# The first norm's root applied behind the input projection, with x and the first unit's weights loaded in column blocks

## What is computed

```python
xn = rmsnorm(x, norm_mix)     # x * rsqrt(mean(x*x, -1) + 1e-6) * gain: one root per token
p = xn @ w_in                 # 2048 x 6400, 52 MB of weights
pA, pB, pC, pD = split(p)     # 1792, 1536, 1536, 1536 columns
pA = pA + (shift_right(pA) - pA) * mu          # token shift, then split in r, k, v, w_lo, a_lo, g_lo
decay = f(tanh(w_lo) @ w2 + w0); a = sigmoid(a_lo @ a2 + a0); g = sigmoid(g_lo) @ g2
kk = k * k_k; kk = kk / max(sqrt(sum(kk*kk) per head), 1e-12)
yA = rwkv7 scan(r, decay, k, v, kk, a) * g     # computed in chunks of 64 tokens
yB = band attention(pB); yC = differential attention(pC); yD = b * conv3(c * h)   # pD = b, c, h
x = x + concat(yA, yB, yC, yD) @ w_out
x = x + mixture of 32 experts(rmsnorm(x))      # 201 MB of expert weights
return rmsnorm(x, norm_final)
```

## Time and profile before

| | |
|---|---|
| median of three runs | 940.85 us (940.47 to 941.32) |
| the profiled execution, its own time | 940.73 us |
| its span, from the first to the last instruction | 938.8 us |
| mean granted clock of TensorE, as a share of full speed | 0.926 |
| busy: PE | 787.3 us (84%) |
| busy: DVE | 432.1 us (46%) |
| busy: ACT | 280.6 us (30%) |
| busy: POOL | 73.5 us (8%) |
| read from HBM | 280 MB, 303 GB/s over the span |

### The profile page before, as it was taken

How to read it: one execution, slowest core, us unless ns; L and a number is a source line. 1 busy time by engine, 2 the same in 40 slices (tenths; PEclk the granted TensorE clock), 3 DMA queues, 4 the chain that set the end, 5 groups by cost and what they waited for, 6 DMA issues and landing times.

```text
span 938.8 us, 18498 instructions
## 1 busy us (share of the span) xinstructions
PE 787.3 (84%) x8182; PEld 634.4 (68%) x8182; DVE 432.1 (46%) x709; ACT 280.6 (30%) x458; POOL 73.5 (8%) x79
## 2 busy tenths in 40 slices
PE   7999999999999999999999774686646856559654
PEld 7999999999999999888877452353523534236322
DVE  6758947654676576854552513113231122311403
ACT  6455543433355666455510101000010000100014
POOL 3110003241000100600000000000000000000002
PEclk9999999999999999999999978797887978979878
DMA  9695544334344545999899999999999999999995
GB/s 302 208 284 159 177 134 137 120 110 135 108 147 153 148 147 180 349 347 365 287 341 404 427 427 429 427 426 428 427 427 427 427 429 426 426 428 427 427 403 203
DMA packets 84655, 285.83 MB, mean 304 GB/s; under 512 B 3818, under 2 KB 55284, under 8 KB 72156
## 3 DMA queue, kind: packets, MB, share of 16 engines
q1 hardware_dynamic: 82304, 278.93, 77.0%
q0 software_dynamic: 1568, 4.02, 1.7%
q10 hardware_dynamic: 700, 1.65, 0.5%
HBM read 280.37 MB, written 4.22 MB: 303 GB/s over the span
## 4 chain that ended last, share of the span: by engine, by line
PE 59%; DMA 33%; DVE 3%; ACT 2%; issue 1%; SPq 1%; POOL 1%; ACTq 0%; POOLq 0%; DVEq 0%
PE bank L1046 26%; DMA arena<-in_expert_w_up 12%; DMA arena<-in_expert_w_down 10%; DMA arena<-in_expert_w_gate 9%; PE bank L1510 8%; PE bank L1590 3%; PE bank L1063 3%; PE bank L1065 3%; PE bank L1064 3%; PE bank L965 2%; PE bank L1475 2%; DMA arena<-in_norm_final 1%; PE bank L1209 1%; DVE ring_r L1715 1%; PE bank L1016 1%
## 5 line engine op out<-in xcount | busy, mean ns | idle before, releaser
L1046 PE MATMUL bank<-xTr,hi 128*128 128x256 f32 x1280 | 235.7, 286 | 0.3 <-DVE ring_r L1715 0.2
L1510 PE MATMUL bank<-arena 128*32 128x256 f32 x2048 | 144.0, 449 | 104.5 <-DMA arena<-in_expert_w_up 60.8
L1046 PEld LDWEIGHTS bank<-xTr,hi 128*128 128x128 f32 x1280 | 199.2, 192 | 5.4 <-issue 3.3
L1715 DVE TENSOR_TENSOR ring_r<-arena,hi 128x1024 fp32r<-128x1024 f32 x132 | 161.9, 1236 | 88.0 <-ACT hi L654 85.5
L1510 PEld LDWEIGHTS bank<-arena 128*32 128x32 f32 x2048 | 80.3, 129 | 165.8 <-issue 138.4
L1046 PE MATMUL bank<-xTr,ring_r 128*128 128x256 f32 x640 | 181.0, 283 | 0.0
L654 ACT ACTIVATE hi<-arena 128x1024 fp32r<-128x1024 f32 x132 | 138.9, 1062 | 111.5 <-PE bank L1046 84.1
L1046 PEld LDWEIGHTS bank<-xTr,ring_r 128*128 128x128 f32 x640 | 122.7, 192 | 0.0
L2149 DVE TENSOR_TENSOR arena<-arena,bank 128x512 f32<-128x512 f32 x56 | 57.8, 1092 | 75.2 <-PE bank L1486 75.2
L895 ACT ACTIVATE g<-bank,coef 128x256 f32<-128x256 f32 x8 | 3.8, 473 | 256.0 <-PE bank L1510 256.0
L1590 PE MATMUL bank<-arena,const 128*32 128x512 f32 x448 | 54.6, 643 | 14.4 <-DMA arena<-in_expert_w_down 14.4
(11 more groups left out here) (338 smaller groups left out, 884.6 us busy)
## 6 DMA issues: line engine op xcount, KB each, us to landing
arena<-in_expert_w_gate SPq DMA_DIRECT2D x30, 2048.0 KB, 30.1
arena<-in_expert_w_up SPq DMA_DIRECT2D x29, 2048.0 KB, 31.8
arena<-in_w_in SPq DMA_DIRECT2D x50, 1024.0 KB, 5.3
arena<-in_expert_w_down SPq DMA_DIRECT2D x24, 2048.0 KB, 30.1
arena<-in_w_out SPq DMA_DIRECT2D x16, 1024.0 KB, 6.0
arena<-in_expert_w_down SPq DMA_DIRECT2D x16, 512.0 KB, 9.1
arena<-in_expert_w_down SPq DMA_DIRECT2D x8, 1024.0 KB, 15.6
arena<-in_expert_w_up SPq DMA_DIRECT2D x6, 1024.0 KB, 7.1
```

Source lines behind the costliest of these rows:

```text
L1046: ins = MM(PJ[n % 2][:, h * U:(h + 1) * U], a, b, start=h + q + tt + k == 0, stop=h == 1 and q == 3 and tt == 3 and k == 2)
L1510: ins = MM(gu[slots_of(a), u * EH:(u + 1) * EH], xg[:, t, slots_of(a)], slot(NUQ * h + NCG * u + a)[:, t * EH:(t + 1) * EH], start=t == 0, ...
L1715: TT(ring_r[:, n % 2, q, :], ring[:, n % 2, q, :], hi[:, g % NHI, :].bitcast(f32), ALU.subtract).then_inc(s["lo_done"], 1)
```

## The change

**At the start.** SP loads the identity first (ScalarE did before), then x in four blocks of 512 columns over all 256 tokens, and behind each block the quarter of unit 0's weights that goes with it (before: three loads of x, then two halves of unit 0). x is no longer scaled. TensorE has 52 fillers, no longer 78, and transposes each block of x when it lands: two blocks ahead of granule 0, one behind granule 0 and one behind granule 1. The gain is loaded and transposed by itself; the other parameters are transposed behind unit 0.

**The root.** The four passes that square x now stand behind unit 0's splits: on both engines between splits 4, 5 and 6. GpSimd issues its eleven loads first, when the transposes are done, and takes the roots after that. VectorE multiplies the identity by the roots (`diag`), and TensorE multiplies a matrix of ones by the result behind granule 5, which gives each token's root in every partition; VectorE copies that to R.

**Applying it.** Bank n is copied to SBUF (`raw` for units 0 to 6), and GpSimd multiplies it by R in place (`scale(n)`), for units 0 to 6, for the q and k parts of both attentions, and for part of D. For the four units that lie with tokens on the partitions the copy itself takes the root as its scale, in two halves. For three units of D VectorE's copy multiplies by R. `keep` and `mix` of units 0 to 6 now read `raw` in SBUF, behind GpSimd, and each stands one or more splits later; `mix` has its own split ahead of it. Nothing changes in the projection's matmuls, in w_out, or in the experts.

The core of the diff:

```diff
@@ SP
-            sp.dma_start(xs[:, 0, :], x_v[0]).then_inc(x_ld[0], 16)
-            for n, part in ((1, slice(0, DM // 2)), (2, slice(DM // 2, DM))):
-                sp.dma_start(xs[:, 1, part], x_v[1][:, part]).then_inc(x_ld[n], 16)
+            sp.dma_start(const[:, 0:P], A["const"][:, 0:P]).then_inc(const_ld, 16)
+            for q in range(4):
+                cols_ = slice(q * 512, (q + 1) * 512)
+                sp.dma_start(xs[:, :, cols_], x_cols[:, :, cols_]).then_inc(x_ld[q], 16)
+                sp.dma_start(ring[:, 0, q, :].rearrange("p (t c) -> p t c", t=4),
+                             w_in_v[:, 4 * q:4 * q + 4, order[0] * U:(order[0] + 1) * U]).then_inc(part_ld[q], 16)
@@ GpSimd
+            pool.wait_ge(s["xt_ready"], 8)
+            for dst, src in loads:
+                pool.dma_start(dst, src).then_inc(par_ld, 16)
             rsqrt(st[:, 0:1])
             rsqrt(st[:, 1:2])
-            for dst, src in loads:
-                pool.dma_start(dst, src).then_inc(par_ld, 16)
+            def scale(n):
+                pool.wait_ge(s["pj_evac"], n + 1)
...
+                    by = R[:, :].unsqueeze(1).to_broadcast([P, 2, SEQ])
+                step(G.tensor_tensor(t, t, by, ALU.mult), s["pj_scaled"])
@@ ScalarE
             def keep(n):
-                act.wait_ge(s["gran_used"], 4 * n + 4)
+                act.wait_ge(s["pj_scaled"], n + 1)
...
-                    A_(mA[:, i, :], PJ[n % 2][:, h * SEQ:(h + 1) * SEQ], ACT.Copy,
+                    A_(mA[:, i, :], raw[n % 2][:, h, :], ACT.Copy,
...
+            for q in range(4):
+                x_high(2 * q)
+                x_high(2 * q + 1)
+                split_hi()
+            split_hi()
+            square(0)
+            split_hi()
+            square(1)
+            split_hi()
@@ TensorE
-            warm(26)
...
+            x_block(0)
+            x_block(1)
             for q in range(4):
                 first_high(q)
                 first_low(q)
-                if q == 0:
-                    x_transpose(7, 0)
-                    x_transpose(7, 1).then_inc(s["xt_ready"], 1)
+                if q < 2:
+                    x_block(q + 2)
...
-            granules(4)
+            granules(2)
+            pe.wait_ge(s["diag_done"], NM)
+            pe.wait_ge(s["pool_ones"], 3)
+            for m in range(NM):
+                ins = MM(K[2][:, m * P:(m + 1) * P], ones_f, diag[:, m, :], start=True, stop=True)
+            ins.then_inc(s["ones_ps"], 1)
+            granules(2)
@@ VectorE
             def mix(n):
+                split_lo(1)
                 for h in range(2):
...
-                    step(STT(mA[:, i, 1:], PJ[n % 2][:, h * SEQ:(h + 1) * SEQ - 1], mu[:, i:i + 1], mA[:, i, 1:],
+                    step(STT(mA[:, i, 1:], raw[n % 2][:, h, 0:SEQ - 1], mu[:, i:i + 1], mA[:, i, 1:],
                              ALU.mult, ALU.add), s["mixA"])
```

More of the change, by code:

```diff
@@ L383, in store_x2 @@
                 sp.dma_start(x2_cols[:, :, nb * 512:(nb + 1) * 512], x2b[nb % 3]).then_inc(x2_st[nb], 16)
-            for n in range(NU_IN + NU_OUT):
+            for n in range(1, NU_IN + NU_OUT):
                 for half in range(2):
@@ L525, in _ @@
             pool.dma_start(gnb[:, :], bc(A["rwkv_gn_b"][0])).then_inc(par3_ld, 16)
+            for n in range(3, NA + 2):
+                scale(n)
             pool.wait_ge(s["gram_ev"], 8)
@@ L545, in _ @@
                      s["gnw_done"])
-            for m in range(NM):
-                rsqrt(st[:, 24:32])
+            for n in (9, 10, 13, 14):
+                scale(n)
+            rsqrt(st[:, 24:32])
+            scale(15)
+            rsqrt(st[:, 24:32])
+            scale(16)
             pool.wait_ge(s["sm_done"], sm_count(NBH - 1))
@@ L552, in _ @@
             pool.dma_start(rw[:, :, NGR:36], A["router_expert_w"].rearrange("l (t p) g -> p (l t) g", t=KT)).then_inc(par2_ld, 16)
-            for i in range(NCH):
+            scale(19)
+            scale(20)
+            rsqrt(cst[:, :, 1:2])
+            scale(21)
+            for i in range(1, NCH):
                 rsqrt(cst[:, :, 1:2])
-            pool.wait_ge(s["pj_evac"], 3 + 19 - NA)
             b_, c_, h_ = (Dq[:, 0, i] for i in range(3))
@@ L696, in _ @@
                         bias=w0h[:, c:c + 1], scale=0.5), s["lora_ev"])
+            keep(2)
             for c in range(AT):
@@ L702, in _ @@
             advance(4)
-            keep(3)
+            evac(3)
             step(A_(lam[:, 2:4], lam[:, 0:2], ACT.Exp), s["lam_exp"])
@@ L722, in _ @@
             advance(1)
+            evac(5)
+            advance(1)
             keep(5)
+            advance(3)
+            evac(6)
+            advance(1)
+            keep(6)
             advance(4)
-            keep(6)
-            advance(5)
             for i in range(6):
@@ L1716, in split_lo, with square @@
                        ALU.subtract).then_inc(s["lo_done"], 1)
+                    if q == 3 and NA + 15 <= n - 1 < NU_IN - 1:
+                        evac(n - 1)
+            def square(h):
+                half = slice(h * DM // 2, (h + 1) * DM // 2)
+                step(V.tensor_tensor_reduce(xsq[:, 1, half], xs[:, 1, half], xs[:, 1, half], 1.0, 0.0, ALU.mult, ALU.add,
+                                            st[:, 1 + 2 * h:2 + 2 * h]))
             def mix(n):
+                split_lo(1)
                 for h in range(2):
@@ L1722, in mix @@
                     v.wait_ge(s["mix1"], 2 * n + 2)
-                    step(STT(mA[:, i, 1:], PJ[n % 2][:, h * SEQ:(h + 1) * SEQ - 1], mu[:, i:i + 1], mA[:, i, 1:],
+                    step(STT(mA[:, i, 1:], raw[n % 2][:, h, 0:SEQ - 1], mu[:, i:i + 1], mA[:, i, 1:],
                              ALU.mult, ALU.add), s["mixA"])
-            for b in range(8):
-                x_low(b)
-                if b % 2 == 1 and b < 2 * LEAD:
-                    split_lo(1)
-            split_lo(4)
+            for q in range(4):
+                x_low(2 * q)
+                x_low(2 * q + 1)
+                split_lo(1)
+            split_lo(1)
+            square(0)
+            split_lo(1)
+            square(1)
+            split_lo(1)
+            v.wait_ge(s["sq1_done"], 2)
+            step(TT(st[:, 0:NM], st[:, 0:NM], st[:, NM:2 * NM], ALU.add))
+            for m in range(NM):
+                variance(m)
+            for m in range(NM):
+                v.wait_ge(s["rstd_done"], m + 1)
+                step(TS(diag[:, m, :], ident, st[:, m:m + 1], None, ALU.mult), s["diag_done"])
+            v.wait_ge(gain_ld, 16 * NVECS + 2)
+            step(TS(omu[:, :], mu, -1.0, 1.0, ALU.mult, ALU.add), s["prep"])
+            step(TS(w0h, w0h, 0.5, None, ALU.mult), s["prep"])
+            step(TS(a0h, a0h, 0.5, None, ALU.mult), s["prep"])
+            step(TS(ok_a[:, :], k_a, -1.0, 1.0, ALU.mult, ALU.add), s["prep"])
+            v.wait_ge(s["ones_ps"], 1)
+            step(V.tensor_copy(R[:, :], K[2][:, 0:SEQ]), s["prep"])
             mix(0)
@@ L1839, in _ @@
                 if i in (1, 2):
-                    step(V.memset(S[i - 1], 0.0), s["halves_zero"])
+                    step(V.memset(S[i - 1], 0.0), s["diag_done"])
                 if i == 3:
```

226 lines of the change are left out of this document (110 added, 116 removed).

## The result

The changed kernel took 948.15 us (median of 4 runs, 947.45 to 949.37), the kernel before 941.09 us beside it. The ratio is 1.0077, with a 95% interval of 1.006 to 1.0095: slower by 7 us, where 941.7 and a range of 938.7 to 944.5 had been predicted. The profiled execution took 947.45 us around a span of 945.6, 6.8 us more than the span before.

What follows compares the result with a forecast made beforehand. The prediction took TensorE's progress from 15 to 500 us as the bound, with a DMA stretch behind it; 940.73 - 3.8 (head start) + 4.5 (lora step and after) + 0.3 (port) = 941.7 us, range 938.7 to 944.5.

Steps and rivals of the forecast that it cites:

- The head start: At the kernel's start: unit 1 begins 4.4 us earlier on TensorE, of which 3.8 us are left after the lora step.
- the diagonal's matmuls: Root's two new matmuls in unit 1: the root is ready 0.2 us before TensorE arrives; they cost 0.35 us.
- Rivals C and D: C: unit 1's second weights land late, 943.9, chance 0.10; D: first granule at most 3 us earlier, 943, chance 0.07.
- the second quarter of x: Load at the start: lands at 7.7 us, before it is wanted at 8.5 to 9.
- the bound that the prediction named: At the start: four copies of x and the first weight split let the first granule begin at about 9.7 us.
- The lora step: Side engines' order around 55 to 98 us: split 17 comes 3.8 us later on VectorE, all lost, not below 3.4.
- The `keep`: Unit 2's keep between ScalarE's two tanh groups at the lora step: moves split 15 by 0.73 us.
- the sum: Whole kernel: 940.73 less 3.8 gained, plus 4.5 lost, plus 0.3 for the shared port, gives 941.7 us.
- Up to granule 26: From the lora step to granule 26 (98.42 us before): 4.5 us lost in all, between 3.6 and 6.
- The port: GpSimd and two-input VectorE passes in SBUF exclude each other: up to 1.1 us late each; 0.3 counted, for unit 4.
- rival B: Slower: two or three port collisions in units 0, 1, 4 and 5 cost 1.5 to 2 us more, 943.5; chance 0.18.
- at nothing: Other copies, scaling passes and multiplications, 15 to 500 us: no cost; if cover failed once, one pass, 0.7 to 1.3.

Runs made afterwards that it cites:

- e1: The changed kernel with the old order at the lora step on ScalarE and VectorE: 943.55 us, ratio 1.0031 to the kernel before.
- e3: The kernel before with unit 2's mix, products and square moved behind split 15 on VectorE, one split ahead of the memset: 945.26 us, ratio 1.0052.
- e12: A reordered whole-computation version of the changed kernel, with 14 filler matmuls added ahead of the bonus matmuls: 937.78 us, ratio 0.9971 to the kernel before.
- e2: The changed kernel with GpSimd multiplying only one column of each half bank for units 3 to 6: 942.73 us, ratio 1.0025 to the kernel before.
- e8: The changed kernel with GpSimd's passes for units 7 and 8 waiting for VectorE's scan preparation: 945.77 us, ratio 1.0042 to the kernel before.

## Why the prediction was wrong

**The head start was right, its path in part.** First granule at 9.75 (9.7 said), unit 1 at 23.36 (23.2), the diagonal's matmuls with no wait, and 3.4 us left at the lora step (3.8 said). Rivals C and D did not occur. But the second quarter of x, put at 7.7 and wanted at 8.5 to 9, held TensorE's transposes for 1.48 us, until 8.90. It cost next to nothing because the copies and the first split, the bound that the prediction named, ended at 9.60. In the other ten traces with this start the first granule began at 9.65 to 10.56.

**The lora step was right as a wait.** 3.8 us were said. 1.07 + 2.40 = 3.5 came as waits, by the order that was named, and some 0.4 in small gaps. e1 and e3 show it from both sides. (The `keep` moved split 15 by 0.84 us, as long as it is in the earlier trace rows, and not by 0.73.)

**The failed step is the sum's silence on TensorE's clock.** The sum took a wait at its own length, and it had a row that should have warned: the earlier trace rows shows 1.00 up to 500 us for a TensorE that is nearly never idle there, and 0.84 behind, where it waits. Behind the wait at granule 17 the clock took 1.3 us, from the bonus matmuls on 1.8. The profiled execution came 5.8 us above the forecast (6.8 us more than before, 1.0 said), and the clock is about 3.0 of that; the median lies 0.7 us higher still. e3 and e12 show it, and the rows of e2. Of the two, the 1.3 us are not sure to come: in e2 and e8 the same wait had no such price.

**A second step failed: the count ended too early.** Up to granule 26 it was close: 4.5 us were said, and 0.3 for the port, and 4.9 came without the clock. I took the chain as over there, at 98 us, where the chain of before had its last visible wait. VectorE's preparation went on to 117 us, with 1.7 us to spare before, and those were used up. So 1.5 us more were lost at the bonus matmuls, which the sum had at nothing.

**The port was mis-sized.** It stood in the sum with 0.3 for unit 4, which came (the split at 84.12), and in rival B with 1.5 to 2 more, counted in units 0, 1, 4 and 5. It decided in 5, 6 and 7: 0.8 + 0.9 + 1.1 us on VectorE's chain, of which 1.3 reached TensorE as a wait, plus the clock behind it. Unit 7's pass I had put under "at nothing", since its own consumer comes late. Its consumer does; what it holds up does not. The reading of the earlier trace rows was also loose: from 203.16 to the split's end are 1.08 us, 0.1 less than the shortest of its like; the rule is borne out by e2 and e8, not by that row.

How far TensorE was behind, step by step: 3.4 us ahead at the lora step, 3.85 lost up to granule 17, 1.3 by the clock, 1.1 at granule 24, 1.5 at the bonus matmuls, 1.8 from there to the end of the transposes, nearly all clock, 0.75 later, together 6.8. Of the last 0.75 the cause was not looked for by a run.

## What to carry to other kernels

When an engine that was never idle has to wait, this can cost more than the wait's length, because the clock may fall behind it; here that was 1.3 to 1.8 us on top, or nothing. Count it as a risk, and fill a wait that can't be taken away with matmuls that nobody needs. A head start is worth only the slack of the engine that must follow, so follow that engine's chain to its last consumer, not to the last wait seen. Work given to an idle engine is free only if what it touches is too: ask what it lies over, not who waits for it.
